# Two-layer hybrid decoder trunk on one core: where the modulation tiles of the third and fourth block are taken in the opening

## What is computed

```python
cond = jax.nn.silu(c)
for layer in range(DEPTH):
    mod = cond @ ada_w[layer] + ada_b[layer]
    shift, scale, gate = jnp.split(mod, 3, axis=-1)
    h = rms_norm(x, norm_w[layer]) * (1.0 + scale[:, None, :]) + shift[:, None, :]
    ...
    proj = h @ w_in
    ...
    x = x + gate[:, None, :] * y
```

## Time and profile before

| | |
|---|---|
| median of 3 runs | 1510.91 us (1507.14 to 1511.65) |
| the profiled execution | 1509.05 us |
| its span in the profile | 1507.2 us |
| PE busy | 1455.9 us, 97% |
| DVE busy | 1103.8 us, 73% |
| ACT busy | 745.4 us, 49% |
| transfers | 361.46 MB, 240 GB/s over the span, up to 387 GB/s in the opening |
| mean granted clock of PE | 0.992 of full speed |

### The profile page before, as it was taken

How to read it: one execution, slowest core, us unless ns; L and a number is a source line. 1 busy time by engine, 2 the same in 40 slices (tenths; PEclk the granted TensorE clock), 3 DMA queues, 4 the chain that set the end, 5 groups by cost and what they waited for, 6 DMA issues and landing times.

```text
span 1507.2 us, 19079 instructions
## 1 busy us (share of the span) xinstructions
PE 1455.9 (97%) x6692; PEld 1203.5 (80%) x6692; DVE 1103.8 (73%) x1233; ACT 745.4 (49%) x1002; POOL 44.2 (3%) x80
## 2 busy tenths in 40 slices
PE   5889999999999989999999999999999999999998
PEld 4667878888888867778888888888888888888886
DVE  5989899989898876878766566566566666666656
ACT  4544646454445455554544544544554454554452
POOL 0000110001000000010000000000000000000000
PEclk9999999999999999999999999999999999999999
DMA  9999889998989745798766566556566566566553
GB/s 346 387 386 387 273 283 336 318 336 278 329 299 352 264 124 182 250 325 293 251 188 187 171 193 183 176 185 191 169 194 183 177 189 190 168 193 190 174 182 111
DMA packets 198613, 361.46 MB, mean 240 GB/s; under 512 B 14252, under 2 KB 47492, under 8 KB 198552
## 3 DMA queue, kind: packets, MB, share of 16 engines
q1 hardware_dynamic: 197832, 359.23, 72.1%
q0 software_dynamic: 304, 1.06, 0.2%
q10 hardware_dynamic: 416, 0.37, 0.1%
HBM read 358.51 MB, written 2.11 MB: 239 GB/s over the span
## 4 chain that ended last, share of the span: by engine, by line
PE 86%; DVE 6%; issue 3%; DMA 3%; ACT 2%; SPq 0%; POOL 0%; DVEq 0%; ACTq 0%; POOLq 0%
PE proj L1373 25%; PE proj L1375 25%; PE proj L1374 25%; DVE ada_acc L882 3%; PE mix L1373 2%; DMA raw<-in_att_w_in 2%; PE mix L1375 2%; PE mix L1374 2%; DVE w_lo L863 1%; PE mix L1507 1%; DMA ada_more<-in_ada_w 1%; PE mix L1584 1%; ACT w_hi L585 1%; PE mix L1632 1%; PE mix L1551 1%
## 5 line engine op out<-in xcount | busy, mean ns | idle before, releaser
L585 ACT ACTIVATE w_hi<-raw 128x1024 fp32r<-128x1024 f32 x480 | 507.9, 1061 | 687.6 <-PE proj L1375 583.9
L863 DVE TENSOR_TENSOR w_lo<-raw,w_hi 128x1024 fp32r<-128x1024 f32 x480 | 585.6, 1222 | 354.4 <-ACT w_hi L585 353.7
L1373 PE MATMUL proj<-w_hi,h_hi 128*128 128x512 f32 x1472 | 582.9, 396 | 4.9 <-DVE w_lo L863 3.0
L1375 PE MATMUL proj<-w_hi,h_lo 128*128 128x512 f32 x1472 | 574.4, 390 | 0.0
L1374 PE MATMUL proj<-w_lo,h_hi 128*128 128x512 f32 x1472 | 573.8, 390 | 0.0
L1373 PEld LDWEIGHTS proj<-w_hi,h_hi 128*128 128x128 f32 x1472 | 276.8, 188 | 65.7 <-issue 8.1
L1375 PEld LDWEIGHTS proj<-w_hi,h_lo 128*128 128x128 f32 x1472 | 276.6, 188 | 58.5
L1374 PEld LDWEIGHTS proj<-w_lo,h_hi 128*128 128x128 f32 x1472 | 277.0, 188 | 57.4 <-issue 1.4
L882 DVE SCALAR_TENSOR_TENSOR ada_acc<-ada_raw,cond,ada_acc 128x1024 f32<-128x1024 f32 x147 | 187.6, 1276 | 5.2 <-DMA ada_raw<-in_ada_w 4.1
L1373 PE MATMUL proj<-w_hi,y_hi 128*128 128x512 f32 x320 | 125.9, 394 | 1.3 <-DVE stream L1043 1.3
L1375 PE MATMUL proj<-w_hi,y_lo 128*128 128x512 f32 x320 | 124.6, 389 | 0.0
(11 more groups left out here) (213 smaller groups left out, 954.5 us busy)
## 6 DMA issues: line engine op xcount, KB each, us to landing
raw<-in_mlstm_w_in SPq DMA_DIRECT2D x192, 512.0 KB, 3.7
ada_raw<-in_ada_w SPq DMA_DIRECT2D x160, 512.0 KB, 5.9
raw<-in_att_w_in SPq DMA_DIRECT2D x128, 512.0 KB, 7.2
raw<-in_mlstm_w_in SPq DMA_DIRECT2D x128, 256.0 KB, 3.0
raw<-in_mlstm_w_out SPq DMA_DIRECT2D x64, 512.0 KB, 4.0
raw<-in_att_w_out SPq DMA_DIRECT2D x32, 512.0 KB, 5.9
ada_more<-in_ada_w SPq DMA_DIRECT2D x16, 512.0 KB, 11.4
work<-in_ada_w SPq DMA_DIRECT2D x16, 512.0 KB, 11.3
```

The lines of the kernel that those rows point to most:

```text
L585: act.activation(w_hi[:, c % LEAD, :], raw[:, c % LEAD, :], ACT.Copy).then_inc(hi_ready, 1)
L863: dve.tensor_tensor(w_lo[:, c % LEAD, :], raw[:, c % LEAD, :], w_hi[:, c % LEAD, :].bitcast(F32), ALU.subtract).then_inc(lo_ready, 1)
L1373: pe.matmul(out_, a_hi, b_hi, start=start, stop=False, **kw)
L1375: return pe.matmul(out_, a_lo, b_hi, start=False, stop=stop, **kw)
```

## The change

One line is changed, the table of `takes0`:

```diff
-            spans = ((-LEAD, 14, KT), (9, 2, 5), (11, 10, 11), (21, 2, 5), (23, 13, 11), (40, 103, 6 * KT))
+            spans = ((-LEAD, 14, KT), (9, 1, 3), (11, 10, 13), (22, 14, KT), (40, 103, 6 * KT))
```

## The result

The changed kernel took 1517.76 us in the median (1516.93 to 1521.89), the kernel before 1510.88 us (1507.14 to 1511.65). The ratio is 1.0057, with a 95% interval of 1.0047 to 1.0067. It is formed from all runs and is not the quotient of the two medians, which would be 1.0046. So the change is 6.9 us slower by the medians and 8.6 us by the ratio, with an interval of 7.1 to 10.1 us: with six runs each, no more can be said than 7 to 10 us. The profiled execution took 1518.6 us with a span of 1516.8 us, 9.6 us over the span of before; of these 9.6 us, 1.8 come from the profiled execution of before, which was that much faster than its median.

The account below looks back on a forecast made before the run. The opening was taken as bound by DVE in places. Second sum later 1.7, third-sum wait 2.7 and clock fall 1.7 sum to 6.1 us, giving 1515.2 from the profiled execution or 1517.0 from the median; forecast 1516, range 1510 to 1520.

Parts of the forecast that it names:

- my own case: The forecast itself: the changed kernel 5 to 7 us slower, chance 0.55.
- a longer low clock: Rival: more waits at granule 29 or 34, or a longer low clock, 8 to 10 us slower; chance 0.08.
- The hidden time behind the first sum: Third block: two takes leave DVE's otherwise unused time before w_lo 16; last take and second sum 1.7 us later.
- The pair's price: On DVE, a take right behind a take costs 1.38 us start to start, against 1.20 behind w_lo.
- The fourth block: Granules 21 to 36: take 63 ends at 165.0 in the old times, PE idle 2.7 us before the third sum.
- The loads cost nothing: SP's queue: weight tiles passing two or three modulation loads cost nothing, since w_lo 16 and 27 wait for ACT's h.
- The clock, 1.7 us: Behind the third sum: one new fall of TensorE's clock, 1.7 us, bounds 0 and twice that.
- The wait that was harmless: Ahead of granule 5: 2.54 us of idle time without a clock fall, cited for a rival without a new fall.
- the first rival: No new clock fall, or DVE's list a microsecond shorter than counted: 4.4 us slower, about 1514; chance 0.22.
- DVE catches up: Rival: DVE gains in its waits, PE's idle time covers the rest: 0 to 2 us slower, 1511 to 1513; chance 0.10.
- the clock doesn't fall: Rival: no new clock fall at the third sum, 1.7 + 2.7 = 4.4 us slower, about 1514; chance 0.22.
- the earlier weight tiles decide: Rival: transfers ahead of w_hi 16 to 21 delay z_add; passing two loads gives 7.9 us faster, 1503; chance 0.05.

Follow-up runs that it names:

- even_but_hidden: Kernel before, fourth block's first three takes kept at place 21, its 13 others in even steps over 22 to 35: 1510.12 us, ratio 1.0001.
- takes_only: Kernel before with DVE's takes in the change's order, SP's loads in the old order: 1518.30 us, ratio 1.0058.
- fourth_only: Kernel before with only the fourth block as in the change, the third as before: 1513.96 us, ratio 1.0032.
- third_only: Kernel before with only the third block as in the change, the fourth as before: 1511.85 us, ratio 1.0016.
- fill_third_wait: The change plus two unused matmuls on PE ahead of the third sum's wait: 1515.06 us, ratio 1.0034 to the kernel before.
- three_at_10: Kernel before with a third take of the third block at place 10, moved from place 11: 1508.55 us, ratio 0.9991.
- loads_behind_15: Kernel before, third block's first three takes and loads at place 10 instead of 9, the 13 others from 11 to 20: 1509.21 us, ratio 0.9991.

## Why the prediction was right

Forecast were 1516 us, in 1510 to 1520; measured were 1517.76 us, and the forecast case, slower by over 0.3%, came true. The waits came where the sum had them. The term of the clock was too small, so the loss of 7 to 10 us lies above my 6.1. By the medians it is still in my own case of 5 to 7 us; by the ratio (8.6) and the profiled execution (9.6) it is in that of the rival "a longer low clock", 8 to 10 us. By its steps:

- *The hidden time behind the first sum.* Right to about a tenth in the profiled execution: w_lo 16 at 89.10, z_add at 106.47 for 106.5, granule 19 idle for 4.35 us for 4.3, second sum at 119.68 for 119.8. even_but_hidden shows the same mechanism for the fourth block by taking it away.
- *The pair's price.* 1.38 us again (99.23 to 100.61). The rule of the Trainium skill ("VectorE: DVE Perf Modes", section "The DRAIN you can't avoid"), that the semaphore costs nothing extra, was measured there on a row of copies and does not carry over to two takes in a row here. Each take reads the sum that the one before wrote, and waits for it; they start 0.18 us farther apart than a take and the w_lo behind it (1.20 us). No run here tells whether the semaphore or the reading of the result costs this.
- *The fourth block.* From w_lo 27 to the end of take 63 I had 39.7 us, measured were 39.5 (128.61 to 168.11). PE waited 2.05 us, not 2.7, because PE had itself become later. takes_only and fourth_only show 2.07. The wait of granule 34 that I allowed for is 0.17 us.
- *The loads cost nothing.* Right within the intervals, shown by takes_only against the change.
- *The clock, 1.7 us.* **This term was too small.** The profiled execution lost 5.2 us more by it than before, 3.4 of them in the new fall at the third sum and 1.7 in a longer fall behind the second sum. takes_only, with the same order of takes, lost 3.4 us more than before: 1.7 at the third sum, and 1.7 in a longer fall behind granule 19. In the profiled execution the narrow matmuls of both sums stand partly in the low stretch, and take 2.41 and 3.14 us instead of 1.92 and 1.84. Behind the second sum the clock was low to 127.9, and that was not PE's loss alone. Granule 22 released its slot late, so ACT made w_hi 27 and DVE w_lo 27 late:

```profile
127.51 1.06 ACT L585 ACTIVATE w_hi<-raw 128x1024 fp32r<-128x1024 f32 x1 [1.08 <-PE proj L1375]
...
128.61 1.23 DVE L863 TENSOR_TENSOR w_lo<-raw,w_hi 128x1024 fp32r<-128x1024 f32 x1 [3.42 <-ACT w_hi L585]
```

w_lo 27 is 3.3 us later than in the earlier trace rows, where my sum had 1.7. Since DVE had no slack from there on, this went straight to the third sum. How long the clock stays low behind the same wait differs between executions. Behind the second sum, 3.4 us were lost in the profiled execution of the change. In third_only, whose takes up to there are the change's, the sum took 1.92 us, at full speed, and 1.7 us were lost behind it; in fill_third_wait, with the same takes again, none. So a single profile doesn't give the price of a fall, and that the median moved by only 6.9 us, near my 6.1, is partly luck.

- *The wait that was harmless.* That the clock did not fall after 2.54 us of idle time ahead of granule 5 was true of that execution, and I used it as evidence for the first rival. It holds for the change as well (2.45 us). But in the eight other profiles with 2.44 to 2.72 us of idle time at this place, the clock fell behind it each time. So in third_only (PE's timeline; a matmul takes 0.39 us at full speed):

```profile
57.88 0.47 PE L1373 MATMUL mix<-w_hi,h_hi 128*128 128x512 f32 x1 [2.58 <-issue]
...
59.22 0.63 PE L1374 MATMUL mix<-w_lo,h_hi 128*128 128x512 f32 x1
```


Of the rivals, "DVE catches up" fell with fourth_only, "the clock doesn't fall" with the windows, and "the earlier weight tiles decide" with takes_only. Still open is how much of the 2.4 us that three_at_10 and loads_behind_15 gain at the second sum reaches the end: the runs allow all of it and nearly none. It is open too whether the change costs nearer to 7 or to 10 us, since every execution has its own falls of the clock.

## What to carry to other kernels

A burst that looks untidy may stand exactly where an engine has nothing else to do. Before work is spread evenly, look in that engine's timeline for what ends the wait behind the burst: here w_lo 16 and w_lo 27 waited for ACT in any case, and five takes in front of them were free. Moved to where DVE had next to no slack, they cost their length less what waits DVE still had there (1.03 us before w_lo 24, 1.76 us before w_lo 35 and 36), and a fall of the clock besides. Price a new wait of TensorE with the clock: the slowed matmuls release their buffers late, and that can set back the engine that caused the wait.

## What the runs showed of the hardware that I had not expected

The clock can be held by work that is of no use: two unused matmuls in a wait of 2 us gave back 2.0 us by the medians and 3.5 by the ratios. The kernel before has such matmuls itself, six around the sum of its first block (L1515, from 30.5 to 39.7 us), and they are no sure cure: in ten of the twelve profiles the clock was low for a time between 35 and 45 us all the same. The Trainium skill ("TensorE: Matmul & The Clock Gate", section "HAM oscillation — how this bites in real kernels") has waits bring the low clock. In this case's traces that is so for the third sum: 1.84 us of narrow matmuls without a wait ahead of them kept the clock, and with 2.05 us of waiting ahead it fell, to 0.50 in the window from 170 to 175 (windows of 0.73 and 0.66 in fourth_only and takes_only, with 2.07 us). At the second sum it is not regular: 1.54 us of waiting were followed by a fall in the kernel before and by none in fill_third_wait. Filling a wait did not help everywhere: the same two matmuls ahead of the second sum gained nothing, where DVE's waits came next.
